# A hybrid decoder step on one core: the output projection started under the last attention heads, decode products shared with GpSimd, pages loaded by SyncE

## The reference

```python
def forget_attend(q, c_q, q_pos, k, v, c_k, k_pos):
    logits = jnp.einsum('nqhd,nkhd->nhqk', q, k).astype(jnp.float32) * (FA_HEAD_DIM ** -0.5)
    decay = jnp.swapaxes(c_q, 1, 2)[..., :, None] - jnp.swapaxes(c_k, 1, 2)[..., None, :]
    causal = k_pos[None, :] <= q_pos[:, None]
    logits = jnp.where(causal, logits + decay, -jnp.inf)
    p = jax.nn.softmax(logits, axis=-1)
    return jnp.einsum('nhqk,nkhd->nqhd', p.astype(v.dtype), v)
...
    o = jnp.swapaxes(o, 0, 1).reshape(n, s, FA_WIDTH)
    return (o * jax.nn.silu(z)) @ w_out + b_out
...
    k_past = cache_k[page_table].reshape(db, -1, FA_HEADS, FA_HEAD_DIM)
    v_past = cache_v[page_table].reshape(db, -1, FA_HEADS, FA_HEAD_DIM)
```

## Time and profile before

| what | value |
|---|---|
| median of 3 runs | 1916.28 us |
| profiled execution, its time and its span | 1924.45 us, 1922.9 us |
| PE busy | 1788.8 us, 93% |
| DVE busy | 1004.8 us, 52% |
| ACT, POOL busy | 670.8 us, 405.9 us |
| DMA moved | 180.43 MB, mean 94 GB/s |

### The profile page before, as it was taken

One profiled execution on the slowest core, in us unless ns is written; L12 is line 12 of the kernel. 1 busy time (PEld: TensorE's weight loads), 2 busy tenths in 40 slices (PEclk: granted clock), 3 DMA queues, 4 the chain that ended last, 5 costly groups with the idle time before them and its releaser, 6 DMA issues.

```text
span 1922.9 us, 28230 instructions
## 1 busy us (share of the span) xinstructions
PE 1788.8 (93%) x10256; PEld 1551.5 (81%) x10256; DVE 1004.8 (52%) x1486; ACT 670.8 (35%) x1022; POOL 405.9 (21%) x424
## 2 busy tenths in 40 slices
PE   5999989999999969998699999999999998769798
PEld 3999989999999969998577888778787876547643
DVE  6432264443545472255524656565646555699662
ACT  5311122222222262154332644545453635342220
POOL 0000011110111000012212342425252324353120
PEclk8999999999999989999799999999999999689998
...
GB/s 321 44 44 44 33 88 77 67 87 76 83 62 84 78 44 108 95 141 107 65 103 66 45 67 52 68 55 55 76 33 87 26 94 68 78 122 301 165 411 35
DMA packets 50190, 180.43 MB, mean 94 GB/s; under 512 B 6522, under 2 KB 8186, under 8 KB 48850
## 3 DMA queue, kind: packets, MB, share of 16 engines
...
...
## 4 chain that ended last, share of the span: by engine, by line
PE 75%; DVE 11%; ACT 5%; issue 5%; POOL 2%; DMA 1%; DVEq 0%; ACTq 0%; SPq 0%; POOLq 0%
PE bank L1634 18%; PE bank L1636 17%; PE bank L1635 17%; PE bank L2072 3%; PE bank L1801 3%; PE bank L1871 2%; PE bank L1922 2%; PE bank L1738 2%; PE bank L1901 1%; PE bank L1902 1%; PE bank L1924 1%; PE bank L1923 1%; POOL p_lo L529 1%; DVE pages L1357 1%; ACT parg L898 1%
## 5 line engine op out<-in xcount | busy, mean ns | idle before, releaser
L1634 PE MATMUL bank<-h_hi,w_lo 128*128 128x344 f32 x1152 | 372.5, 323 | 0.7 <-DVE w_lo L1010 0.5
L1635 PE MATMUL bank<-h_lo,w_hi 128*128 128x344 f32 x1152 | 367.5, 319 | 0.0
L1636 PE MATMUL bank<-h_hi,w_hi 128*128 128x344 f32 x1152 | 367.3, 319 | 0.0
L529 POOL TENSOR_TENSOR p_lo<-parg,p_hi 128x512 fp32r<-128x512 f32 (+1 forms) x192 | 204.4, 1079 | 216.3 <-ACT p_hi L900 214.6
L1634 PE MATMUL bank<-x_hi,w_lo 128*128 128x512 f32 x528 | 225.1, 426 | 7.5 <-POOL x_lo L486 6.4
L1634 PEld LDWEIGHTS bank<-h_hi,w_lo 128*128 128x128 f32 x1152 | 216.6, 188 | 1.7 <-DVE w_lo L1010 0.8
L1635 PEld LDWEIGHTS bank<-h_lo,w_hi 128*128 128x128 f32 x1152 | 216.7, 188 | 0.5 <-issue 0.5
L1636 PEld LDWEIGHTS bank<-h_hi,w_hi 128*128 128x128 f32 x1152 | 216.4, 188 | 0.0
L1636 PE MATMUL bank<-x_hi,w_hi 128*128 128x512 f32 x528 | 212.4, 402 | 0.0
L1635 PE MATMUL bank<-x_lo,w_hi 128*128 128x512 f32 x528 | 212.1, 402 | 0.0
L1634 PE MATMUL bank<-y_hi,w_lo 128*128 128x320 f32 (+2 forms) x512 | 177.8, 347 | 26.6 <-ACT y_hi L721 9.1
...
## 6 DMA issues: line engine op xcount, KB each, us to landing
...
```

The source lines that it names most:

```text
L529: g.tensor_tensor(p_lo[:, r, off:HALF], parg[:, r, off:HALF], p_hi[:, r, off:HALF].bitcast(F32), ALU.subtract).then_inc(S("p_ready"), 1)
L1634: mm(out, lhs_lo, rhs_hi, start=first, stop=False)
L1635: mm(out, lhs_hi, rhs_lo, start=False, stop=False)
L1636: return mm(out, lhs_hi, rhs_hi, start=False, stop=last)
```

## The change

The work is the same. What moves:

- PE runs the first 12 steps of block 0 of the output projection (k 0 to 5, both halves) inside the last `phase` (`early`), one after another between its score matmuls; then, behind the phase, k 6 of block 0, k 0 to 6 of block 1, and k 7 of both. Blocks 0 and 1 take four banks of PSUM instead of two.
- ACT makes `y2_hi` 0 to 5 at the start of the last phase, and `w_hi` of unit U_FA+1 and `y2_hi` 6 in its middle. `y2_lo` 0 to 5 are made by POOL, in place of y2T; 6 is made by DVE in the phase, with `w_lo` of U_FA+1; 7 by DVE behind it.
- Key and value pages are issued by SP, in its order with weights and residuals: key set b+2 comes behind residual b and ahead of the weights of block b+1.
- From the third sequence on, POOL multiplies pages 1 and 3 of each set, DVE pages 0 and 2; all sums stay on DVE. POOL's loops over sequences are written out.
- Places in SBUF are exchanged to make room. The decay pages and query rows stay on POOL's queue.

```diff
-        y2_hi = at("y2_hi", [P, KB, T], F32R, R1 + 32768)
-        y2_lo = at("y2_lo", [P, KB, T], F32R, R2 + 32768)
-        r2T = at("r2T", [P, KB, T], F32, R1)
+        y2_hi = at("y2_hi", [P, KB, T], F32R, R2 + 32768)
+        y2_lo = at("y2_lo", [P, KB, T], F32R, R1)
+        r2T = at("r2T", [P, KB, T], F32, R1 + 32768)
...
             load(U_FA + 1, (U_FA + 1) % 2)
+            def load_keys(b):
+                for p in range(NP):
+                    page = sp.value_load(ptab[0:1, bass.ds(b * NP + p, 1)], min_val=0, max_val=cache_k.shape[0] - 1)
+                    sp.dma_start(pages[:, b % 2, p, :], cache_k[bass.ds(page, 1), :, :].rearrange("a p c -> p (a c)"))\
+                      .then_inc(S(f"pages_in{b % 2}"), 16)
+            def load_values(b):
+                if b < 2:
+                    sp.wait_ge(S("pages_used"), NS - 1 + b)
+                elif b == 2:
+                    sp.wait_ge(S("fa_mm"), 2 * KB)
+                elif b >= 4:
+                    sp.wait_ge(S("pages_used"), NS + b - 3)
+                for p in range(NP):
+                    page = sp.value_load(ptab[0:1, bass.ds(b * NP + p, 1)], min_val=0, max_val=cache_v.shape[0] - 1)
+                    sp.dma_start(pages[:, b % 4, p, :], cache_v[bass.ds(page, 1), :, :].rearrange("a p c -> p (a c)"))\
+                      .then_inc(S(f"pages_in{b % 4}"), 16)
             load_swapped(KB - 1)
+            sp.wait_ge(S("table_in"), 16)
+            sp.wait_ge(S("mm"), 12 * KB)
+            load_keys(0)
...
             sp.wait_ge(S("pv_done"), 24 * KB)
...
+                if b + 2 < NS:
+                    sp.wait_ge(S("pages_used"), b + 1)
+                    load_keys(b + 2)
+            load_values(0)
+            load_values(1)
             sp.dma_start(g_row[:, :], ln_rows[0:1, :].broadcast_to([P, D])).then_inc(S("rows_in"), 16)
             sp.dma_start(b_row[:, :], ln_rows[1:2, :].broadcast_to([P, D])).then_inc(S("rows_in"), 16)
+            load_values(2)
+            load_values(3)
             sp.wait_ge(S("r2_ready"), 2 * KB)
             sp.wait_ge(S("lo_ready"), U_FS)
...
-                wait(pool, S("qk_prod"), NP * (b - 1))
-                settle(pool, S("settled"))
-                row = scr_q[b:b + 1, :] if isinstance(b, int) else scr_q[bass.ds(b, 1), :]
-                pool.dma_start(qbs[s][:, :], row.broadcast_to([P, D])).then_inc(S(f"qb_in{s}"), 16)
-            load_set(cache_k, 0, 0)
+                if b >= 2:
+                    pool.wait_ge(S("qk_prod"), NP * (b - 1) if b < 4 else 2 * NP + 2 * (b - 3))
+                    wait(pool, S("qk_pool"), 2 * (b - 3))
+                pool.dma_start(qbs[s][:, :], scr_q[b:b + 1, :].broadcast_to([P, D])).then_inc(S(f"qb_in{s}"), 16)
+            def product(b, p):
+                if p == 1:
+                    pool.wait_ge(S(f"pages_in{b % 2}"), 16 * NP * (b // 2 + 1))
+                    pool.wait_ge(S(f"qb_in{b % 2}"), 16 * (b // 2 + 1))
+                g.tensor_tensor(pages[:, b % 2, p, :], pages[:, b % 2, p, :], qbs[b % 2][:, :], ALU.mult)\
+                    .then_inc(S("qk_pool"), 1)
+            def y2_low(k):
+                pool.wait_ge(S("y2_hi"), k + 1)
+                g.tensor_tensor(y2_lo[:, k, :], y2T[:, k, :], y2_hi[:, k, :].bitcast(F32), ALU.subtract)\
+                    .then_inc(S("y2_split"), 1)
...
+            y2_low(4)
+            y2_low(5)
             p_low(KB - 1, 0)
             pool.wait_ge(S("nl_ready"), 16 * KB)
             load_q(0, 0)
...
-            for b in range(NS):
-                if b < 2:
-                    pool.wait_ge(S("pages_used"), NS - 1 + b)
-                elif b == 2:
-                    pool.wait_ge(S("fa_mm"), 2 * KB)
-                elif b >= 4:
-                    pool.wait_ge(S("pages_used"), NS + b - 3)
-                load_set(cache_v, b, b % 4)
+            for b in range(2, NS):
+                load_q(b, b % 2)
+                load_f(b)
+                product(b, 1)
+                product(b, 3)
             for name, n in (("vn_out", 16), ("k_out", 16 * KB), ("v_out", 16 * KB), ("kqv_s_out", 16)):
...
                 act.wait_ge(S("o_step"), 8 * k + 8)
-                A(y2_hi[:, (k + 6) % KB, :], y2T[:, k, :], ACT.Copy).then_inc(S("y2_hi"), 1)
+                if k == 0:
+                    act.wait_ge(S("mm"), 12 * KB)
...
                     evac(j + 1, 0, 0)
+                else:
+                    for k in range(KB - 2):
+                        y2_high(k)
...
                     split_hi(j + 2, 0)
+                else:
+                    hi(U_FA + 1, (U_FA + 1) % 2, (U_FA + 1) // 2 + 1, "mm", 12 * KB)
...
-            act.wait_ge(S("k_out"), 16 * KB)
-            act.wait_ge(S("kq_lo"), 4 * KB)
...
-            for k in range(KB):
-                y2_high(k)
+            y2_high(KB - 1)
             for b in range(KB):
-                if b + 1 < KB:
...
                     dve.wait_ge(S(f"qb_in{b % 2}"), 16 * (b // 2 + 1))
-                v.tensor_tensor(pages[:, b % 2, p, :], pages[:, b % 2, p, :], qbs[b % 2][:, :], ALU.mult)\
-                    .then_inc(S("qk_prod"), 1)
-                dve.wait_ge(S("qk_prod"), n + 1)
+                if by_pool(b, p):
+                    dve.wait_ge(S("qk_pool"), 2 * (b - 2) + (p + 1) // 2)
+                else:
+                    v.tensor_tensor(pages[:, b % 2, p, :], pages[:, b % 2, p, :], qbs[b % 2][:, :], ALU.mult)\
+                        .then_inc(S("qk_prod"), 1)
+                    dve.wait_ge(S("qk_prod"), n + 1 if b < 2 else 2 * NP + 2 * (b - 2) + p // 2 + 1)
                 last = v.tensor_reduce(scol[:, p, b, :], pages[:, b % 2, p, :].rearrange("p (h d) -> p h d", d=HD), AX.X, ALU.add)
...
                 else:
+                    dve.wait_ge(S("v_out"), 16 * KB)
...
                     score(2)
+                    lo(U_FA + 1, (U_FA + 1) % 2)
...
                 if not more:
+                    y2_low(KB - 2)
...
                 phase(j, True)
+            gates(1, "fa_b_out")
...
-            gates(1, "fa_b_out")
-            for k in range(KB):
-                y2_low(k)
+            y2_low(KB - 1)
             for n in range(6, EARLY):
...
+            def fa_step(b, half, k):
+                slot = (U_FA + b) % 2
+                cs = slice(half * HALF, half * HALF + HALF)
+                if k == 0 and half == 0:
+                    pe.wait_ge(S("lo_ready"), U_FA + b + 1)
+                    if b == 0:
+                        pe.wait_ge(S("tok_ready"), 1)
+                        pe.wait_ge(S("zs_done"), 4 * KB)
+                    if b == 1:
+                        pe.wait_ge(S("arg_ready"), 24 * KB)
+                if k == 0 and b >= 2:
+                    pe.wait_ge(S("fg2_ready"), 2 * b + half - 3)
+                if b == 0 and half == 0:
+                    pe.wait_ge(S("y2_split"), k + 1) if k < KB - 2 else pe.wait_ge(S("y2_last"), k - KB + 3)
+                last = three(fa_bank(b, half), w_hi[:, slot, k, :], w_lo[:, slot, k, :],
+                             y2_hi[:, k, cs], y2_lo[:, k, cs], k == 0, k == KB - 1)
+                if k == KB - 1:
+                    last.then_inc(S("fa_mm"), 1)
...
                             step(j + 1, n // 16, n % 16)
+                def early(n):
+                    if not more:
...
                 steps(14, 17)
+                early(0)
                 peak(j, 5)
                 steps(17, 20)
+                early(1)
                 peak(j, 6)
                 steps(20, 23)
+                early(2)
                 peak(j, 7)
                 steps(23, 27)
...
+            for half in range(2):
+                fa_step(0, half, KB - 2)
+            for half in range(2):
+                for k in range(KB - 1):
+                    fa_step(1, half, k)
             for b in range(KB):
-                slot = (U_FA + b) % 2
-                pe.wait_ge(S("lo_ready"), U_FA + b + 1)
                 for half in range(2):
-                    cs = slice(half * HALF, half * HALF + HALF)
-                    wait(pe, S("fg2_ready"), 2 * b + half - 1)
-                    for k in range(KB):
-                        if b == 0 and half == 0:
-                            pe.wait_ge(S("y2_split"), k + 1)
-                        last = three(bank(half), w_hi[:, slot, k, :], w_lo[:, slot, k, :],
-                                     y2_hi[:, (k + 6) % KB, cs], y2_lo[:, k, cs], k == 0, k == KB - 1)
-                    last.then_inc(S("fa_mm"), 1)
+                    for k in range(KB - 1 if b < 2 else 0, KB):
+                        fa_step(b, half, k)
                 if b == 4:
```

69 lines of the change are left out of this document (39 added, 30 removed).

## The result

The changed kernel takes 1929.06 us (median of five runs, 1923.90 to 1930.06), the kernel before 1916.28 (1913.56 to 1917.02): a ratio of 1.0055, 95% interval 1.0038 to 1.0071. It is slower by 12.8 us, where 7 us less were forecast.

The account below looks back on a forecast made before the run. DVE was taken to bound projection blocks 0 to 3, PE the later ones. Gains of -7.8 by the projection's end, +3.0 in the last pair included, and +0.8 for exclusion gave -7.0: 1909.3 us from 1916.28, range 1901 to 1919.

Parts of the forecast that it names:

- about 12: Before block 2 of the projection: PE idle for about 12 us, released by `w_lo`.
- both its chains: Block 2's start: VectorE free at 1728.3, weights landed on SyncE's queue at about 1730; start at 1732.4 against 1737.20.
- The last pair, +3.0 forecast: Last head pair: 2.6 for two VectorE operations, +1.5 for `early`, -1.1 for a shorter wait; bounds -1 and +8.
- at the start of the phase, where both wait for the peaks: Last pair: where work taken over by ScalarE and GpSimd (six `y2_hi`, six `y2_lo` at 2.38 each) was said to lie.
- priced at 2.6: Last pair: `w_lo` and one `y2_lo` on VectorE, both on the chain, 1.3 us each.
- priced at +1.5: Last pair: the 36 matmuls of `early`, up to 4.0 us longer against some 1.5 saved by a faster PE clock.
- the wait for the decode copies: PE's wait of 3.31 us at the turn, forecast to shrink by 1.22 with one VectorE product ahead of it gone.
- the 10 forecast: Output projection: -10 us forecast for its length.
- The term was +0.8 us: Projection: cost of GpSimd's products to VectorE's operations, +0.8 us in all for three blocks, bounds 0 and +10.8.
- The row of 1.51 against 1.22 us: Profile row: a VectorE score product overlapped by a GpSimd subtraction; taken as at most 0.3 us for each such operation.
- rival D: Slower: DVE and GpSimd exclude each other, blocks take 14.6 instead of 10.9 us; +5.6, so 1921.9; chance 0.12.
- +13.4: Rival D's exclusion cost: 11.0 us over three blocks and +2.4 for block 2's start, set against -7.8.

Follow-up runs that it names:

- e2: Changed kernel with GpSimd's first four `y2_lo` held until VectorE's first cast of the peaks is done: 1924.32 us, ratio 1.0028 to the kernel before.
- e12: e3 with VectorE's `w_lo` of block 1 and `y2_lo` 6 behind the last `gate_o`, not inside the last pair: 1910.05 us, ratio 0.9971.
- e11: e3 with no steps of block 0 inside the last pair, all 14 behind it: 1918.74 us, ratio 1.0015.
- e9: e8 with all products on VectorE, none on GpSimd: 1914.02 us, ratio 0.9986.
- e5: e3 with all products on VectorE, page loads still on SyncE: 1913.72 us, ratio 0.9979.
- e1: Changed kernel with the weights of block b+1 issued ahead of key set b+2 on SyncE: 1917.71 us, ratio 1.0008 to the kernel before.
- e3: Changed kernel with both edits, weights ahead of key pages on SyncE and `y2_lo` behind the first cast: 1913.66 us, ratio 0.9977.
- e4: Changed kernel with all products on VectorE and key and value pages issued by GpSimd as in the kernel before: 1917.72 us, ratio 0.9998.
- e8: e3 with `w_lo` of block 2 right behind the first `r2T` and the decode copies ahead of two scores: 1910.92 us, ratio 0.9974.
- e14: e12 with the two VectorE order edits of e8 added: 1908.06 us, ratio 0.9953 to the kernel before.

## Why the prediction was wrong

**Up to block 5 it was right in kind.** The 7.89 us of PE idle time are gone, PE waits before block 2 (10.7, forecast "about 12"), blocks 2 to 5 start 13.1, 11.2 and 14.7 us apart (12.5, 10.9 and 14.5), the wait for `ex` is 1.25 us shorter (1.22), and the end is unchanged. Block 2's start is right in both its chains, and in part by luck: VectorE was 2.6 us later than forecast, since its product beside GpSimd took 3.37 us, and so it came just when ScalarE was done with `w_hi` (1730.86), whose weights were as late as forecast.

**The last pair, +3.0 forecast, +8.0 measured.** The step that failed first is the sentence that GpSimd's six `y2_lo` lie "at the start of the phase, where both wait for the peaks". VectorE has a cast there, which the `y2_lo` block: 5.7 us of the pair in the changed kernel's trace, 4.7 of the time by e2. The text asked only what ScalarE and GpSimd wait for, not what VectorE runs beside them. The rest of the pair is then 2.3 us longer, near the +3.0, but not for the reasons given: `w_lo` and `y2_lo` 6, priced at 2.6, are 4.4 (e12), because `w_lo` is itself blocked, and the matmuls of `early`, priced at +1.5, seem to have cost less; in e11 the pair without them is 2.1 longer. Pairs with the same instructions differ by up to 5 us between profiled executions (78.2 in e9, 83.2 in e5, with a PE clock of 0.83 and 0.79), so the sign of that last term stays open; the medians of e2, e11 and e12 point the same way as the traces.

**Blocks 5 and 6, the largest failure.** The text took 1.22 us off the wait for the decode copies; it grew by 10.5. I followed the weights of block 2 down SyncE's queue, past key set 3, but not those of the later blocks, where the key set in front must wait for scores. And I asked only when PE needs block 6's weights, not what stands in order behind VectorE's own wait for them. e1 shows it: 11.4 us, and the wait falls from 13.84 to 2.05. With that mended the projection is 6.6 us shorter than before, against the 10 forecast.

**Exclusion between GpSimd and VectorE.** The term was +0.8 us; the operations lose 14.1 us in the projection. The row of 1.51 against 1.22 us was read as a price for each operation beside GpSimd; but VectorE's product there overlapped only the last 0.4 us of the first of the two GpSimd operations, and the second, which came while it ran, was the one that paid: 1.64 us instead of 0.82. It says nothing of full overlap. The Trainium skill, "SBUF — State Buffer", section "Who interferes with whom", was right here: casts, `tensor_scalar` and operations with both inputs in SBUF wait (0.17 to 5.87, 0.20 to 2.31, 1.22 to 3.40 us), sums don't (1.2). My rival D had this mechanism, in the blocks only, at +5.6 us. There its price was lower: the products' gain cancelled it (e3 and e5 alike), and D's blocks of 14.6 us did not come; with the weights early (e3) blocks 2 to 4 start 13.9 and 13.1 us apart, though, not 12.5 and 10.9. The text's upper bound of the term, +10.8, doesn't fit D's own +13.4 either. So D's direction was right, but for a reason that it did not have: of the loss of 12.8 us, 11.4 are the queue and 4.7 the `y2_lo` (exclusion, but in the pair), and what is left is a gain of 3.

**What the change was worth.** The rebuilt end alone: nothing (e4, ratio 0.9998). Pages on SyncE: 4 to 7 us once the weights are ahead. Products on GpSimd: 0, 3 and 5 us in three orders (e3, e8, e14), of which only the last is nearly clear of noise; why it depends on the order isn't shown.
